# Cross attention's product with the values: three passes of rounded halves in place of float32, and one buffer for the probabilities

## The reference

```
mk = (mem_prompt @ xa_wk[l]).reshape(bp, N_MEM, H_X, HD_X)
mv = (mem_prompt @ xa_wv[l]).reshape(bp, N_MEM, H_X, HD_X)
...
q = (h @ wq).reshape(b, t, H_X, HD_X)
s = jnp.einsum('bthd,bmhd->bhtm', q, mk) * (HD_X ** -0.5)
p = jax.nn.softmax(s, axis=-1)
o = jnp.einsum('bhtm,bmhd->bthd', p, mv)
return o.reshape(b, t, D_MODEL) @ wo
```

## Time and profile before

| | |
|---|---|
| median of 3 runs | 3334.53 us (3330.86 to 3337.27) |
| the profiled execution | 3332.01 us, its span 3330.2 us |
| busy in the span | TensorE 3180.8 us (96%), VectorE 1897.3 (57%), ScalarE 766.6 (23%), GpSimd 778.3 (23%) |
| mean granted TensorE clock | 0.981 of full speed |

### The profile page before, as it was taken

How to read it: one execution, slowest core, us unless ns; L and a number is a source line. 1 busy time by engine, 2 the same in 40 slices (tenths; PEclk the granted TensorE clock), 3 DMA queues, 4 the chain that set the end, 5 groups by cost and what they waited for, 6 DMA issues and landing times.

```text
span 3330.2 us, 45162 instructions
## 1 busy us (share of the span) xinstructions
PE 3180.8 (96%) x19152; PEld 2953.2 (89%) x19152; DVE 1897.3 (57%) x2816; ACT 766.6 (23%) x1099; POOL 778.3 (23%) x424
## 2 busy tenths in 40 slices
PE   7999897799999999999999999799999999999996
PEld 7888887799589999999998877699579999999996
DVE  5655677552436555554557999652436545554456
ACT  4775222310222111111113222410222111111111
POOL 2211121132023333333332000222013333333331
PEclk9999998899999999999999999999999999999998
DMA  3111445324501111111112110123501111111111
GB/s 135 39 58 45 141 147 178 122 70 152 202 26 49 45 45 51 45 45 47 50 45 58 32 38 13 40 76 129 225 20 49 46 50 45 45 48 49 45 45 71
DMA packets 83644, 238.16 MB, mean 72 GB/s; under 512 B 15723, under 2 KB 20715, under 8 KB 81651
## 3 DMA queue, kind: packets, MB, share of 16 engines
q1 hardware_dynamic: 74962, 217.96, 20.1%
q10 hardware_dynamic: 8480, 17.32, 1.4%
HBM read 217.93 MB, written 17.32 MB: 71 GB/s over the span
## 4 chain that ended last, share of the span: by engine, by line
PE 82%; DVE 14%; issue 2%; ACT 1%; DMA 1%; SPq 0%; DVEq 0%; ACTq 0%
PE ps L473 68%; DVE ca L1374 3%; PE ps L868 2%; PE ps L791 2%; PE ps L779 2%; PE ps L845 2%; DVE tls L1378 1%; DVE X L1370 1%; PE ps L608 1%; PE ps L578 1%; DVE Gl L1370 1%; PE ps L953 1%; PE ps L538 1%; DVE rst L1710 1%; PE ps L598 1%
## 5 line engine op out<-in xcount | busy, mean ns | idle before, releaser
L473 PE MATMUL ps<-Hh,Wh 128*128 128x344 f32 x3552 | 778.4, 328 | 41.8 <-DVE Hl L1370 17.0
L444 POOL CAST Wh<-wraw 128x1024 fp32r<-128x1024 f32 x210 | 224.5, 1069 | 2485.4 <-PE ps L473 2151.7
L473 PE MATMUL ps<-Hl,Wh 128*128 128x344 f32 x3552 | 759.9, 322 | 0.0
L473 PE MATMUL ps<-Hh,Wl 128*128 128x344 f32 x3552 | 756.8, 322 | 0.0
L473 PEld LDWEIGHTS ps<-Hh,Wh 128*128 128x128 f32 x3552 | 604.0, 190 | 69.1 <-issue 33.9
L473 PEld LDWEIGHTS ps<-Hl,Wh 128*128 128x128 f32 x3552 | 606.4, 191 | 0.0
L473 PEld LDWEIGHTS ps<-Hh,Wl 128*128 128x128 f32 x3552 | 598.7, 190 | 0.0
L446 POOL TENSOR_TENSOR Wl<-wraw,Wh 128x1024 fp32r<-128x1024 f32 x210 | 553.6, 2636 | 16.8
L1370 DVE TENSOR_TENSOR X<-ps,X 128x1032 f32<-128x1032 f32 x200 | 244.3, 1229 | 292.7 <-PE ps L473 292.7
L1370 DVE TENSOR_TENSOR ub<-ps,rst_d 128x1032 f32<-128x1032 f32 x88 | 108.4, 1232 | 419.2 <-PE ps L473 236.4
L1000 ACT ACTIVATE cb<-ub,fp 128x1032 f32<-128x1032 f32 x88 | 110.1, 1252 | 968.5 <-DVE ub L1370 968.5
(11 more groups left out here) (264 smaller groups left out, 3364.1 us busy)
## 6 DMA issues: line engine op xcount, KB each, us to landing
wraw<-in_wts SPq DMA_DIRECT2D x224, 512.0 KB, 3.6
cc<-in_cmk SPq DMA_DIRECT2D x16, 1024.0 KB, 9.9
cc<-in_cmv SPq DMA_DIRECT2D x16, 1024.0 KB, 9.6
pg<-in_ck SPq DMA_DIRECT2D x48, 256.0 KB, 2.8
pg<-in_cv SPq DMA_DIRECT2D x48, 256.0 KB, 2.8
mwa<-in_memw SPq DMA_DIRECT2D x16, 512.0 KB, 7.7
mwb<-in_memw SPq DMA_DIRECT2D x16, 512.0 KB, 7.6
X<-in_x SPq DMA_DIRECT2D x6, 1032.0 KB, 6.9
```

The costliest lines, as they stand in the source:

```text
L444: pool.tensor_copy(Wh[:, j, :], wraw[:, j, :]).then_inc(w_hi, 1)
L473: ins = mm(o, w[:, wcol[0], wcol[1]:wcol[1] + P], r, start=first and a == 0, stop=last and a == 2)
```

## The change

The probabilities and the values are each held as a rounded half and a rest, and the product is made in three passes of fp32r: `mvh*pTh + mvh*pTl + mvl*pTh`. ScalarE writes a rounded copy `mvh` and a plain copy `mv` (for the store) of each half of the values, VectorE the rest `mvl` (`low_of_values`). In `turned`, ScalarE rounds both banks to `pTh`, and behind it VectorE subtracts to get `pTl`. To make room, `p` has one buffer: exps(u) waits for turn(u-1). The plain values are stored in two transfers, and ScalarE waits for them before it writes over their place. The core of the diff:

```diff
-        at, _ = layout([("p", [P, 2, 4, MEM]), ("pT", [P, 2, MT, 512]), ("mst", [P, 2, 3, 4])], cr_at)
+        at, _ = layout([("p", [P, 4, MEM]), ("mvl1", [P, MT, 512], F32R), ("pTh", [P, 2, MT, 512], F32R),
+                        ("mst", [P, 2, 3, 4])], cr_at)
+        at.update(layout([("pTl", [P, 2, MT, 512], F32R)], tail)[0])
...
                     for dc in range(2):
+                        c = 2 * hx + dc
                         for m in range(MT):
-                            ins = mm(ps[:, 6 + dc, :], cr["mv"][:, m, (2 * hx + dc) * P:(2 * hx + dc + 1) * P],
-                                     at["pT"][:, u % 2, m, :], start=m == 0, stop=m == MT - 1)
+                            hi = cr["mvh"][:, m, c * P:(c + 1) * P]
+                            lo = mvl[c // 4][:, m, c % 4 * P:(c % 4 + 1) * P]
+                            ph, pl = at["pTh"][:, u % 2, m, :], at["pTl"][:, u % 2, m, :]
+                            for a, (w, p) in enumerate(((hi, ph), (hi, pl), (lo, ph))):
+                                ins = mm(ps[:, 6 + dc, :], w, p, start=m == 0 and a == 0,
+                                         stop=m == MT - 1 and a == 2)
...
                 scores(0)
-                pe.wait_ge(*of_layer(l, "mv_ev", 1))
+                pe.wait_ge(*of_layer(l, "mv_ev", 6))
...
                 for half in range(2):
-                    fn(cr["mv"][:, :, half * 512:(half + 1) * 512], ps[:, 6 - 2 * half:8 - 2 * half, :], ACT.Copy, ss("mv_ev"))
+                    of_half = ps[:, 6 - 2 * half:8 - 2 * half, :]
+                    fn(cr["mvh"][:, :, half * 512:(half + 1) * 512], of_half, ACT.Copy, ss("mv_ev"))
+                    fn(mv[half][:, :, :], of_half, ACT.Copy, ss("mv_ev"))
...
-                act.wait_ge(*of_layer(l, "mv_ev", 2))
-                store(o_mv[l], cr["mv"][:, :, :])
+                act.wait_ge(*of_layer(l, "mv_ev", 6))
+                for half in range(2):
+                    store(o_mv[l, :, :, half * 512:(half + 1) * 512], mv[half][:, :, :])
+                mv_stored = 16 * nstored[0]
...
-                    if u >= 2:
-                        act.wait_ge(*of_layer(l, "x_t", u - 1))
+                    if u:
+                        act.wait_ge(*of_layer(l, "x_t", u))
...
-                    fn(at["pT"][:, u % 2, 0, :], ps[:, 4, :], ACT.Copy, ss("x_pt0"))
+                    fn(at["pTh"][:, u % 2, :, :], ps[:, 4:6, :], ACT.Copy, ss("x_pt0"))
...
+                    if u == 1:
+                        act.wait_ge(stored, mv_stored)
                     out(u - 1)
...
+                def low_of_values(half):
+
+                    dve.wait_ge(*of_layer(l, "mv_ev", 3 * half + 2))
+                    tt_(mvl[half][:, :, :], ps[:, 6 - 2 * half:8 - 2 * half, :],
+                        cr["mvh"][:, :, half * 512:(half + 1) * 512].bitcast(F32), ALU.subtract, ss("mv_ev"))
...
-                    copy(at["pT"][:, u % 2, 1, :], ps[:, 5, :], ss("x_pt1"))
+                    dve.wait_ge(*of_layer(l, "x_pt0", u + 1))
+                    tt_(at["pTl"][:, u % 2, :, :], ps[:, 4:6, :], at["pTh"][:, u % 2, :, :].bitcast(F32),
+                        ALU.subtract, ss("x_pt1"))
```

More of the change, by code:

```diff
@@ L130, in build @@
         Wl = keep("Wl", [P, 2, 1024], F32R)
+        con_at = top[0]
         con = keep("con", [P, NCON])
@@ L183, in build @@
         ha_at = x_at + 4 * KC * N
-        cr, cr_at = layout([("qx", [P, KC, N]), ("mkT", [P, KC, MEM]), ("mv", [P, MT, D])], ha_at)
+        cr, cr_at = layout([("qx", [P, KC, N]), ("mkT", [P, KC, MEM]), ("mvh", [P, MT, D], F32R)], ha_at)
         cr.update(layout([("qtx", [P, D], F32R)], tail)[0])
@@ L188, in build @@
         mws = [nmem["mwa"][:, 0, :], nmem["mwa"][:, 1, :], nmem["mwb"][:, 0, :], nmem["mwb"][:, 1, :]]
-        at, _ = layout([("p", [P, 2, 4, MEM]), ("pT", [P, 2, MT, 512]), ("mst", [P, 2, 3, 4])], cr_at)
+        at, _ = layout([("p", [P, 4, MEM]), ("mvl1", [P, MT, 512], F32R), ("pTh", [P, 2, MT, 512], F32R),
+                        ("mst", [P, 2, 3, 4])], cr_at)
+        at.update(layout([("pTl", [P, 2, MT, 512], F32R)], tail)[0])
+        mvl = [place("mvl0", [P, MT, 512], F32R, con_at + 4 * C_HEAD + 16)[0], at["mvl1"]]
         c3, _ = layout([("cc", [P, RING, MT, D]), ("zc", [P, MT, 32]), ("zst", [32, 4]), ("pr", [32, MEM]),
-                        ("pm", [P, MT * H, NS * NS]), ("ov", [P, 2 * P])], scr + 8 * 1024)
+                        ("pm", [P, MT * H, NS * NS]), ("ov", [P, 2 * P]), ("mv0", [P, MT, 512])],
+                       scr + 8 * 1024)
+        mv = [c3["mv0"], place("mv1", [P, MT, 512], F32, scr)[0]]
         c3["junk2"] = place("junk2", [P, H, HDX], F32, where["rst_d"])[0]
@@ L249, in build @@
         COUNTS = {
-            "ld_mem": 16, **{f"ld_mw_{s}": 64 for s in range(4)}, "mw_used": 16, "mk_ev": KC, "mv_ev": 2,
+            "ld_mem": 16, **{f"ld_mw_{s}": 64 for s in range(4)}, "mw_used": 16, "mk_ev": KC, "mv_ev": 6,
             "x_qt": 1, "x_qtc": 2, "x_e": 32, "x_s": 8, "x_p": 8, "x_t": 8, "x_pt0": 8, "x_pt1": 8, "x_o": 16,
@@ L857, in turn @@
                             ins = pe.transpose(ps[:, 4 + m, tt * P:(tt + 1) * P],
-                                               at["p"][:, u % 2, tt, m * P:(m + 1) * P], ident)
+                                               at["p"][:, tt, m * P:(m + 1) * P], ident)
                     ins.then_inc(ss("x_t"), 1)
@@ L890, in cross @@
                 ins.then_inc(ss("xs_t"), 1)
-                pe.wait_ge(*of_layer(l, "mv_ev", 2))
+                pe.wait_ge(*of_layer(l, "mv_ev", 6))
                 turn(0)
@@ L1217, in cross @@
                     act.wait_ge(*of_layer(l, "mw_used", 8 + 4 * (half + 1)))
-                    fn(cr["mv"][:, :, half * 512:(half + 1) * 512], ps[:, 6 - 2 * half:8 - 2 * half, :], ACT.Copy, ss("mv_ev"))
+                    of_half = ps[:, 6 - 2 * half:8 - 2 * half, :]
+                    fn(cr["mvh"][:, :, half * 512:(half + 1) * 512], of_half, ACT.Copy, ss("mv_ev"))
+                    fn(mv[half][:, :, :], of_half, ACT.Copy, ss("mv_ev"))
                 act.wait_ge(*of_layer(l, "mk_ev", KC))
                 store(o_mk[l], cr["mkT"][:, :, :])
-                act.wait_ge(*of_layer(l, "mv_ev", 2))
-                store(o_mv[l], cr["mv"][:, :, :])
+                act.wait_ge(*of_layer(l, "mv_ev", 6))
+                for half in range(2):
+                    store(o_mv[l, :, :, half * 512:(half + 1) * 512], mv[half][:, :, :])
+                mv_stored = 16 * nstored[0]
                 def exps(u):
                     act.wait_ge(*of_layer(l, "x_m", u + 1))
-                    if u >= 2:
-                        act.wait_ge(*of_layer(l, "x_t", u - 1))
+                    if u:
+                        act.wait_ge(*of_layer(l, "x_t", u))
                     for tt in range(4):
-                        fn(at["p"][:, u % 2, tt, :],
+                        fn(at["p"][:, tt, :],
                            ps[:, (u % 2) * 2 + tt // 2, (tt % 2) * MEM:(tt % 2 + 1) * MEM], ACT.Exp,
@@ L1789, in cross @@
                     .then_inc(ss("xs_soft"), 1)
+                def low_of_values(half):
+                    dve.wait_ge(*of_layer(l, "mv_ev", 3 * half + 2))
+                    tt_(mvl[half][:, :, :], ps[:, 6 - 2 * half:8 - 2 * half, :],
+                        cr["mvh"][:, :, half * 512:(half + 1) * 512].bitcast(F32), ALU.subtract, ss("mv_ev"))
+                low_of_values(0)
                 dve.wait_ge(*of_layer(l, "xs_t", 2))
@@ L1794, in cross @@
                          ps[:, 1, m * 32:(m + 1) * 32].rearrange("p (b h) -> p h b", h=H), ss("xs_soft"))
+                low_of_values(1)
                 def maxima(u):
@@ L1808, in scaled @@
                     dve.wait_ge(*of_layer(l, "x_r", u + 1))
-                    tt_(at["p"][:, u % 2, :, :], at["p"][:, u % 2, :, :],
+                    tt_(at["p"][:, :, :], at["p"][:, :, :],
                         m[:, u % 2, 2, :].unsqueeze(2).broadcast_to((P, 4, MEM)), ALU.mult, ss("x_p"))
```

## The result

| | before | after |
|---|---|---|
| median (range, runs) | 3332.03 us (3324.73 to 3337.27, 10) | 3342.54 us (3339.66 to 3345.41, 10) |
| the profiled execution, its span | 3332.01, 3330.2 | 3344.27, 3342.5 |
| mean granted TensorE clock | 0.981 | 0.978 |

The change costs 10.5 us: the ratio is 1.0032 [1.0023, 1.0041], slower by 0.32%. The median lies within the forecast's range (3329 to 3345), but I had forecast +3.2 us and "no difference that can be told", and it can be told.

What follows compares the result with a forecast made beforehand. TensorE sets the pace within a turn, but its gain becomes idle behind the other engines' chain. Turns +1.4 and cached tile +1.8 make +3.2 us on 3333.3: 3336.5 us, range about 3329 to 3345.

Steps and rivals of the forecast that it cites:

- Weigh: TensorE's product in each turn: twelve fp32r products of 0.2325 us make 2.79 in place of 3.44, 0.65 less.
- The gain turns into idle: Ahead of each turn's transposes: TensorE's saving becomes 0.7 us of idle, waiting for VectorE's p.
- A turn of 7.80: One turn to the next, set by the chain exps, pTh, pTl, out, p: 7.80 us, against TensorE's own 7.11.
- +0.70: From turn(1) to turn(7): six steps make 46.80 us against 46.10 before, per layer.
- The start, +1.28: From turn(0) to turn(1): pTl(0) delays p(1), so turn(1) comes 1.28 us later, per layer.
- The end, -1.28: From turn(7) to the second triple of the output product: 8.73 us in place of 10.01, per layer.
- The clock as a rival: In the turns: TensorE's idle lowers its clock, up to +90 us, 3380 if half the time; chance 0.04.
- The values ahead of the turns: Ahead of the cached products: TensorE waits for all six steps of the values, hidden under scores(0), cost 0.
- The last cached tile, +0.9 a layer: Ahead of scores(1): moved stores make the last cached tile arrive 0.9 us later, bounds 0 to 2.2, +1.8 both layers.
- This rival, the stores: At the wait for the last cached tile: moved stores make it 2.2 late per layer, +8.1 us, 3341; chance 0.16.
- turns above 8.1: Sign against the forecast: turns over 8.1 us apart, where 7.8 was expected.
- a granted clock under 1.00 within the turns: Sign against the forecast: TensorE's granted clock below 1.00 during the turns.

Runs made afterwards that it cites:

- The turned order: Changed kernel with VectorE making the product p(u+1) ahead of pTl(u), and the maxima behind out(u-1); 3328.14 us, ratio 0.9986.
- fewer waits: Changed kernel with two of VectorE's waits ahead of pTl left out, so it waits only for pTh; 3342.02 us, ratio 1.0026.
- the late stores: Changed kernel with the stores of keys and values issued only after TensorE has used the last cached tile; 3337.77 us, ratio 1.0018.
- where TensorE is kept at work: Changed kernel with TensorE making scores(7) a second time, unused, in the idle time ahead of turn(7); 3339.40 us, ratio 1.0024.
- the 4 KB rows: Changed kernel with the values' output laid out by halves, so store rows are 4 KB in place of 2 KB; 3343.65 us, ratio 1.0027.

## Why the prediction was right in its mechanism and too small in its sum

- **Weigh**: 0.2325 for each product predicted, 0.23 measured. Right.
- **The gain turns into idle**: 0.7 ahead of each turn predicted, released by p; 0.65 measured, released by p. The turned order shows the cause by taking it away: TensorE then has no idle in the steady turns, and a turn takes 7.13 (7.11 worked out for TensorE alone). It is VectorE's list, in which p(u+1) stands behind pTl(u), and not the single buffer.
- **A turn of 7.80**: 7.99 measured. pTl took 1.22 to 1.23 and pTh 1.03, as bounded; the handoffs were mis-sized. I took 0.03 from the end of one to the start of the next; ahead of pTl it was 0.14, and fewer waits bring it to 0.04: several waits in a row cost 0.10 here. Ahead of the exponentials it was 910.34 - 909.15 - 1.09 = 0.10, and two buffers for p take 0.08 off the turn, where I had priced the single buffer at 0.01. For six turns the 0.19 makes 1.1 of the 2.18 by which +2.88 exceeds +0.70. The rest lies in the first two steps, 900.90 - 892.12 = 8.78 and 909.15 - 900.90 = 8.25, and it is the clock, for which the working had nothing at turn(1). In the first step TensorE is at its lower level behind the idle ahead of turn(1). In the second the maxima wait 0.37 for scores(3), which TensorE ends late for that reason, and the exponentials start 1.46 behind the turn in place of 1.19: 0.27, about what 8.25 exceeds 7.99 by. In layer 1 of the kernel with the late stores the transposes of turn(1) take 1.09, and the first two steps 7.96 and 7.98.
- **The start, +1.28**: +1.46 measured, by the same handoffs.
- **The end, -1.28**: this step failed, by 2.7 us a layer: +1.42 measured. The chain was right: where TensorE is kept at work the triple comes 8.74 behind turn(7), and 8.73 was predicted. What failed is that the working took every duration at a granted clock of 1.00. I asked for the clock only for the steady turns, where it indeed stays at 1.00. The window of the earlier trace rows that I took for it does reach over the 2.76 of idle ahead of turn(7) of before, but I did not ask what the longer idle there would do: step 7 has no scores, so the 0.65 of a steady turn and the 3.45 of the scores add up to 4.10, and 4.09 was measured.
- **The clock as a rival** had 0.04, as a fall in all turns. It falls at turn(1) and turn(7) of both layers instead, and already ahead of scores(1). What the Trainium skill, "TensorE: Matmul & The Clock Gate", section "A second HAM failure mode: psum-queue depth-cycling", tells of another kernel, read as a rule for this one, would have had the clock swing in the steady turns; the trace does not agree, at 1.00 from 910 to 934 with 0.64 and 0.65 of idle ahead of the transposes.
- **The values ahead of the turns**, 0: right, the cached products start without idle.
- **The last cached tile, +0.9 a layer**: +1.13 and +1.31 measured. With the stores late in both kernels the tile is used at 12.19 and 13.36 with the change and at 11.99 and 13.30 without it: within 0.2, so the delay goes with the stores, as far as one trace of each can tell. scores(1) took 4.43 and 4.32, against 3.72 in layer 0 and 5.91 in layer 1 before: layer 0 lost 0.7 to the clock and layer 1 won 1.6, within the 2.3 that I gave either way. This rival, the stores, had the sign of the result, and its 3341 is close to the 3342.5, but by chance: it had the tile 2.2 late a layer, which was 1.2, and the turns at +0.7, which were +5.7. Moving the stores takes 4.8 us away with the change and 1.6 without it.

Together per layer: the turns +5.7 where +0.7 was worked out, an excess of 5.0 of which the clock at turn(7) is 2.7, the clock at turn(1) about 1.0 and the handoffs about 1.3; the tile +1.2 where +0.9 was. So most of the miss is the clock at two places for which the sum had no term. That 3342.5 lies within the range all the same is luck in part: its width was put there for the tile, for pTl, for the clock at scores(1) and for the spread of the runs, and most of the time went to none of these. Of the signs named, turns above 8.1 (8.78 and 8.25) and a granted clock under 1.00 within the turns (0.89 from 890 to 905) spoke against the working, and weigh(7) starts 949.19 - 941.10 = 8.09 behind turn(7), later than the 6.03 of before and not sooner.

## What to carry to other kernels

When a step becomes cheaper on the engine that bounds, walk the other engines' lists in order and ask which instruction that the bound engine needs stands behind one that it does not need yet: here the place of two calls on VectorE's list was worth 14 us, more than the 10.5 that the change had cost. Work out the longest idle at the ends of a pipeline apart from the steady turns, and price what comes behind it at the lower clock as well as at the full one. A handoff across three waits took 0.14 here and across one 0.04; drop those that another wait already covers.

## What had not been expected of the hardware

The clock does not go by the length of an idle time alone. In the kernel before, 2.76 of idle ahead of turn(7) left the transposes at 1.09 and weigh(6) at 3.60; in the same kernel with its stores late, the same 2.76 made weigh(6) 5.21 and 5.01. Ahead of turn(1), 2.33 of idle made the transposes 1.80 and 1.90 in after, and left them at 1.09 in layer 1 of the kernel with the change and the stores late.

Nor do the transposes alone tell whether it fell. In the kernel with the turned order TensorE idles 2.33 ahead of turn(7) in both layers; in layer 0 the transposes then take 1.62, as above, and in layer 1 1.06, but there the products of weigh(6) behind them step by 2439.76 - 2439.33 = 0.43:

```profile
2437.59 1.06 PE L863 MATMUL ps<-con,p 128*128 128x128 f32 x8 [2.33 <-DVE pTl L1388]
...
2439.33 0.63 PE L879 MATMUL ps<-pTl,mvh 128*128 128x512 f32 x1
2439.76 0.63 PE L879 MATMUL ps<-pTh,mvl 128*128 128x512 f32 x1
```

The granted clock is 0.87 in both layers (931 to 944 and 2435.5 to 2448.5), and the second triple comes 10.28 and 10.63 behind turn(7): it fell in both, in layer 1 a little later.

Idle of 4.0 to 4.1 ahead of turn(7) made the transposes 1.97 in both layers of after, of the two buffers, of the late stores, of the 4 KB rows and of the fewer waits; the 0.54 to 0.67 of the steady turns never did. What decides in between stays open.
